# Experts' one-hot products: one stretch of eight in seven banks instead of three stretches

## The reference, cut to what matters

```
gate, up = jnp.split(xb @ w_gate_up[e], 2, axis=-1)
return (jax.nn.silu(gate) * up) @ w_down[e]
...
y = jax.ops.segment_sum(y_buf[dest] * w_s[:, None], tok_s, num_segments=n_tok)
```

## Time and profile before

| what | us |
|---|---|
| median of three runs | 2835.09 |
| lowest, highest | 2832.41, 2835.9 |
| the profiled execution, whole | 2828.44 |
| its span, first to last instruction | 2826.4 |
| one block of the experts in it | 16.28 |

### The profile page before, as it was taken

How to read it: one execution, slowest core, us unless ns; L and a number is a source line. 1 busy time by engine, 2 the same in 40 slices (tenths; PEclk the granted TensorE clock), 3 DMA queues, 4 the chain that set the end, 5 groups by cost and what they waited for, 6 DMA issues and landing times.

```text
span 2826.4 us, 30173 instructions
## 1 busy us (share of the span) xinstructions
PE 2662.1 (94%) x12198; PEld 1986.2 (70%) x12198; DVE 1517.4 (54%) x2830; ACT 988.6 (35%) x1700; POOL 15.3 (1%) x20
## 2 busy tenths in 40 slices
PE   7989999979997999989999999979989999999998
PEld 5867677633445566668778888758778878778786
DVE  5347655457765398965344544556543233344534
ACT  3234445321213232224233332245744244432222
POOL 0000000000000000000000000000000000000000
PEclk9889999989998999999999999989999999999999
DMA  4311001299973210212213222122212432213120
GB/s 152 81 44 48 31 31 60 91 398 393 413 319 95 79 28 25 90 60 82 98 61 119 90 90 90 46 75 72 77 60 82 108 79 78 87 60 112 68 90 30
DMA packets 178750, 296.02 MB, mean 105 GB/s; under 512 B 26160, under 2 KB 120752, under 8 KB 170416
## 3 DMA queue, kind: packets, MB, share of 16 engines
q1 hardware_dynamic: 175088, 282.52, 28.6%
q0 software_dynamic: 2304, 8.39, 0.8%
q10 hardware_dynamic: 1216, 3.15, 0.3%
HBM read 288.79 MB, written 4.19 MB: 104 GB/s over the span
## 4 chain that ended last, share of the span: by engine, by line
PE 60%; DVE 6%; ACT 3%; issue 1%; DVEq 0%; ACTq 0%
PE ps L317 16%; PE ps L319 16%; PE ps L318 16%; PE ps L325 6%; PE ps L2007 2%; PE ps L331 1%; DVE ps L1932 1%; PE ps L340 1%; PE ps L2104 1%; PE ps L2034 0%; PE ps L384 0%; DVE x L2270 0%; DVE arena L2267 0%; DVE t L355 0%; ACT L2710 0%
## 5 line engine op out<-in xcount | busy, mean ns | idle before, releaser
L303 DVE TENSOR_TENSOR ws0l<-w,ws0h 128x1024 fp32r<-128x1024 f32 (+1 forms) x125 | 135.8, 1087 | 134.1 <-ACT ws0h L295 132.2
L303 DVE TENSOR_TENSOR ws1l<-w,ws1h 128x1024 fp32r<-128x1024 f32 (+2 forms) x125 | 134.9, 1080 | 131.2 <-ACT ws1h L295 131.1
L295 ACT ACTIVATE ws1h<-w 128x1024 fp32r<-128x1024 f32 (+2 forms) x125 | 117.3, 938 | 147.6 <-PE ps L319 142.0
L303 DVE TENSOR_TENSOR ws2l<-w,ws2h 128x1024 fp32r<-128x1024 f32 (+1 forms) x93 | 104.7, 1126 | 99.1 <-ACT ws2h L295 99.0
L295 ACT ACTIVATE ws0h<-w 128x1024 fp32r<-128x1024 f32 (+1 forms) x125 | 117.9, 943 | 103.8 <-PE ps L319 103.8
L1932 DVE SCALAR_TENSOR_TENSOR ps<-arena,ps 128x512 f32<-128x512 f32 x224 | 150.9, 749 | 0.0
L325 PE MATMUL ps<-arena 128*128 128x512 f32 (+11 forms) x440 | 134.7, 482 | 1.6 <-ACT t L752 1.1
L317 PE MATMUL ps<-hpc_hi,ws1h 128*128 128x512 f32 x320 | 128.1, 400 | 6.1 <-DVE ws1l L303 4.0
L317 PE MATMUL ps<-hpc_hi,ws2h 128*128 128x512 f32 x328 | 130.8, 399 | 1.5 <-issue 1.5
L319 PE MATMUL ps<-hpc_hi,ws2l 128*128 128x512 f32 x328 | 128.8, 393 | 0.0
L318 PE MATMUL ps<-hpc_lo,ws2h 128*128 128x512 f32 x328 | 128.8, 393 | 0.0
(11 more groups left out here) (564 smaller groups left out, 6182.3 us busy)
## 6 DMA issues: line engine op xcount, KB each, us to landing
w<-in_w_gate_up SPq DMA_DIRECT2D x32, 2048.0 KB, 12.3
w<-in_w_in SPq DMA_DIRECT2D x37, 1024.0 KB, 5.4
w<-in_w_down SPq DMA_DIRECT2D x32, 1024.0 KB, 12.7
w<-in_w_ff SPq DMA_DIRECT2D x16, 2048.0 KB, 8.2
w<-in_w_in SPq DMA_DIRECT2D x13, 2048.0 KB, 8.3
w<-in_w_in SPq DMA_DIRECT2D x48, 512.0 KB, 5.2
w<-in_w_branch SPq DMA_DIRECT2D x6, 2048.0 KB, 7.8
w<-in_w_out SPq DMA_DIRECT2D x4, 2048.0 KB, 7.6
```

Of the source, the lines that this page charges most:

```text
L295: A_(e).activation(pair_of(t)[0], tiles[t][1], ACT.Copy).then_inc(*e.inc(hi, ("hi", t)))
L303: e.go.tensor_tensor(p[1], tiles[t][1], p[0].bitcast(F32), ALU.subtract).then_inc(*e.inc(lo, ("lo", t)))
```

## The change

The gate/up products of a block run through without a break, and all eight slices of the block before follow in one stretch. They go to seven different banks, 0, 1, 3, 4, 5, 6, 7, and the eighth slice to bank 3 again. As these banks are also those of the token transposes (0, 1) and of the down products (6, 7), `turn_x` and `down` now wait for the adds that empty them. The adds stand in one piece on VectorE, behind `up`, and `place` ahead of `up`.

```diff
+        BACK = [ps[j] for j in (0, 1, 3, 4, 5, 6, 7, 3)]
...
-            def turn_x(bb):
+            def turn_x(bb, before):
                 e.wait_ge(*(in_xg if bb < NMAIN else in_xh)[bb % 2](("x", bb)))
                 for c in range(2):
+                    e.wait_ge(*dv(("xm", before, c)))
                     e.wait_ge(*ev(("x", bb - 1, c)))
...
                 for c in range(2):
                     e.wait_ge(*dv(("y", bb - 1, c)))
+                    e.wait_ge(*dv(("xm", bb - 1, 5 + c)))
...
             def back(bb, d):
 
-                n = 8 * bb + d
                 e.wait_ge(*dv(("onehot", bb)))
-                e.wait_ge(*dv(("y", bb, d // 4)))
-                e.wait_ge(*dv(("xm", (n - 3) // 8, (n - 3) % 8)))
-                products(e, ps[3 + n % 3][:], [(y_[:, P * d:P * d + P], onehot[bb % 2][:]) for y_ in (yo_hi, yo_lo)], ("cb", bb, d))
+                e.wait_ge(*dv(("y", bb, 0 if d < 4 else 1)))
+                e.wait_ge(*(dv(("xm", bb, 2)) if d == 7 else dv(("xm", bb - 1, 7))))
+                products(e, BACK[d][:], [(y_[:, P * d:P * d + P], onehot[bb % 2][:]) for y_ in (yo_hi, yo_lo)], ("cb", bb, d))
...
-            turn_x(b0)
+            turn_x(b0, b0 - 1)
...
-                behind = {2: (0, 1, 2), 5: (3, 4, 5), 7: (6, 7)} if bb > b0 else {}
                 for k in range(8):
                     two_products(e, ps[2], xgT[bb % 2][:, k, :], [moe_w[2 * bb + r][0][1][:, k, :] for r in range(2)],
                                  k == 0, k == 7, ("gu", bb))
-                    for d in behind.get(k, ()):
+                if bb > b0:
+                    for d in range(8):
                         back(bb - 1, d)
...
-                    turn_x(bb + 1)
+                    turn_x(bb + 1, bb - 1)
...
-                e.go.tensor_tensor(x[:, d, :], x[:, d, :], ps[3 + (8 * bb + d) % 3][:], ALU.add).then_inc(*e.inc(dv, ("xm", bb, d)))
+                e.go.tensor_tensor(x[:, d, :], x[:, d, :], BACK[d][:], ALU.add).then_inc(*e.inc(dv, ("xm", bb, d)))
...
-                old = range(8) if bb > b0 else ()
-                for d in old[0:3]:
-                    add(bb - 1, d)
                 if bb + 2 < b1:
                     place(e, bb + 2)
-                for d in old[3:6]:
-                    add(bb - 1, d)
                 up(bb)
-                for d in old[6:8]:
-                    add(bb - 1, d)
+                if bb > b0:
+                    for d in range(8):
+                        add(bb - 1, d)
                 to_tokens(e, bb)
```

## The result

| | before | after |
|---|---|---|
| median, five runs each | 2834.65 | 2819.06 |
| lowest to highest | 2831.55 to 2835.9 | 2818.07 to 2821.64 |
| the profiled execution | 2828.44 | 2821.6 |
| one block of the experts in it | 16.28 | 15.41 |

The ratio of the runs is 0.9953, with an interval of 0.9941 to 0.9965: 13.3 us faster (9.9 to 16.7). The two medians differ by 15.6.

A forecast was written before the change was run, and what follows sets the result against it. TensorE's queue was taken to bound the expert stage; 0.24 and 0.36 us saved a block, 15 times, make 9.0 us, with block 5 and the tail at nothing. From the 2835.09 us median: 2826.1 us, range 2820.5 to 2832.5.

The forecast's parts named there:

- TensorE bounds the stage: Expert blocks: TensorE's queue, busy for all 16.28 us, sets a block's length; a saving there counts 15 times.
- Gate and up: 32 gate/up matmuls per block in one stretch instead of 12 + 12 + 8: 7.27 to 7.03 us, saving 0.24.
- One-hot: 16 one-hot matmuls per block in one stretch instead of 6 + 6 + 4: 4.29 to 3.93 us, saving 0.36.
- the extra 0.10 us on the first one-hot product: Start of every one-hot stretch on TensorE: 0.10 us extra, taken as the reason to price changes of kind from the trace.
- My high bound: Upper bound on the gate/up and one-hot saving together: 0.63 us a block, around a forecast of 0.60.
- `up`: TensorE's small wait for the gated product, 1.4 us over four blocks, goes: ready at 1.0 us, due at 3.8.
- The new waits: One-hot, token-transpose and down products on TensorE find their adds done, the tightest by 0.5 us; slower rival, chance 0.07.
- Block 5: Rotary-table stall moves before the eighth one-hot product but stays: gap 3.7 us, half-clock part 2.8 us unchanged; net 0.
- The clock did not stay up: Rival at block 5: the clock does not fall, gain 11.8 us, time 2823.3 us; chance 0.15.
- The DMA engines: Weight loads need 16.0 us a block but land 9.5 us early; rival that they bind: gain 4.2 us, chance 0.09.
- The sum: Whole kernel: 15 x 0.60 = 9.0 us saved, block 5 and tail 0; 2826.1 us, chance 0.55.
- my upper bound of 12.3: Largest gain allowed for the kernel: 15 x 0.63 + 2.8 us, the 2.8 from a clock that does not fall.

The follow-up runs named there:

- the two- and the eight-stretch kernel: Changed kernel with a block's one-hot products in two stretches of four, or eight of one, instead of one stretch: 2821.5 us, and 2859.51 us (one run).
- the three-bank kernel: Changed kernel's one stretch and VectorE order, but in the three banks of the kernel before: 2831.51 us, ratio to the kernel before 0.9991.
- the banks alone: Kernel before, keeping its three stretches and VectorE order, with the change's seven banks and their waits: 2829.97 us, ratio 0.9984.
- the extra copies: 256 KB more copied to HBM by DMA with each weight half: 2832.81 us in the changed kernel, 2831.6 us in the kernel before.

## Why the prediction was right, and where its sizes were off

**TensorE bounds the stage**: right. Every block of the kernel after except block 5 is 15.41 us with TensorE busy throughout, and the time follows.

**Gate and up, 0.24 forecast, 0.30 measured. One-hot, 0.36 forecast, 0.51 measured.** The mechanism is shown: the two- and the eight-stretch kernel price a pair of changes at 0.37 and 0.36 us, and two pairs are 0.74 of the 0.87. The term that was mis-sized is the steady price of a matmul. (That the extra 0.10 us on the first one-hot product speaks for a change of kind was no proof, as the three-bank kernel shows; and which of the differences between the two kinds makes the price is open.) I took it from the difference of two short stretches (0.87 us for four, 0.2175) and from what two or four spacings left over (0.235). In the long stretches it is (6.97 - 0.07) / 32 = 0.2156 and (3.78 - 0.34 - 0.23) / 14 = 0.229. A few nanoseconds too much on 32 and on 14 matmuls are 0.06 + 0.08 = 0.14 of the 0.27 us a block that were missing. My high bound, 0.63 a block, did not hold the 0.87 either, and it has no working: with the lower of my own two spacings, 0.23, the saving would have been 0.24 + 0.43 = 0.67.

The Trainium skill ("TensorE: Matmul & The Clock Gate", Step-by-step, phase 5), whose rule had no term for a change of kind, does not fit there: the traces show 0.37 us for a pair.

**`up`**: the other 0.13 us that were missing. The prediction said that the small wait for `up` goes, but kept the 0.30 us in front of the transposes and gave it no term. In the kernel before, the last one-hot product was followed after 0.30 us by the transposes, now after 0.23, and the transposes are 0.06 shorter.

**The new waits**: right in every block but the last and, for the eighth product, block 5. The eighth product, the token transposes and the down products found their banks empty; 1.78 us in the adds' way cost 1.58. The slack was smaller than forecast where it was tightest. In block 4 add 5 ends at 665.30 + 5 x 0.60 + 0.68 = 668.98, 4.64 us behind the end of gate and up, and the down products, due 4.96 us behind a first one-hot product that starts 0.08 before that end, are due at 4.88: 0.24 us, not 0.5. In the last block the down products come sooner, as there are no tokens to turn, and wait 0.68; I had not looked at it, and it cost only 0.06, as they had waited 0.56 for ScalarE before.

**Block 5**: right, the gap is 3.88 us (3.7 forecast) before the eighth product, and the clock falls as before. The block is 6.93 us over the others, 6.57 before, so 0.4 us lost. The clock did not stay up in either trace of the change. That it stays down for the same 6.8 us in both kernels was taken over and not worked out: with two stretches it is 3.4 us, and with the banks alone too (granted 0.52 over 690.15 to 693.56). That this part came out is partly luck.

**The DMA engines**: 16.0 us a block forecast, 16.1 measured, and they did not bind, because the lead lasts; 5.4 us are left. That it is the lead which hides them is shown by the pair with the extra copies: where it is gone, TensorE waits. The Trainium skill ("DMA: Bandwidth & Descriptors", Where 436 GB/s comes from) has a ceiling of 435 GB/s for the ports; the fullest windows of a block here show 428, so the traces agree within 2%. The same section has the HBM side bind at about 358 GB/s for transfers like these, and there the traces do not agree.

**The sum**: 9.0 forecast; 12.4 by the stage in the traces; 13.3 by the ratio of the runs. The forecast was right in what gains and what holds it, and about 0.27 us a block too low in size; the stage's 12.4 is already at my upper bound of 12.3, which had counted on a clock that stays up. What the run-to-run spread outside the stage adds can't be told apart at this size.

## What to carry to other kernels

On TensorE, count how often the queue changes between kinds of matmul (here a 64-column pair and a full-width product): a pair of changes costs 0.37 us here, and putting one kind in one stretch wins it back only if there are banks enough for the stretch and the engine that empties them starts early enough.
Price a long stretch from the longest stretch of the trace, not from the difference of short ones.
When the bound engine gets faster, look at how far ahead the loads land and by how much the lead shrinks each turn: a transfer that was nearly free at one period (2.8 us here) may cost the whole gain at the next.

## What the runs showed of the hardware that I had not expected

- A pair of changes costs the same 0.36 to 0.37 us whether the stretch between them has one product or four; where it could be split, 0.15 of it is on the gate/up side and 0.23 on the one-hot side. About 0.10 of the latter also comes behind a wait within one kind.
- With the extra copies, TensorE waited up to 2.99 us at a time for weights, and the profile put it down to "issue", not to a DMA. "No row of TensorE waiting for a DMA", on which the prediction rests in part, is therefore weak evidence; the landing times are the strong one (831.24 for a block that starts at 831.32).
- Leaving out 1.84 us of matmuls gave 0.15 us, so two paths were within 0.2 us of each other, and the busy share (VectorE at 10.96 of 15.41 us in the changed kernel) does not show it.
